# A depthwise convolution as banded products over four phases of time, with its norm and the projection's operand order moved

## The reference

```python
# second layer, after h = rmsnorm(x) * (1 + scale) + shift
proj = h @ w_in                       # q, k, v, index q/k/w, and cu (2 x 512 channels)
attn_out = _dsa_attention(q, k, v, q_idx, k_idx, w_idx)   # top-256 sparse, causal, 8 heads
a, g = split(cu); glu = a * sigmoid(g)                     # 512 channels
y = depthwise_conv(glu, conv_w, taps=31, causal) + conv_b  # y[t,c] = sum_k w[k,c] glu[t-30+k,c]
conv_out = silu(layernorm(y) * conv_norm_g + conv_norm_b)
x = x + gate * (concat([attn_out, conv_out]) @ w_out)      # then the feed-forward part
```

## Time and profile before

| | us |
|---|---|
| median of 3 runs (2816.2 to 2828.43) | 2823.13 |
| the profiled execution's own time | 2835.03 |
| its span, first to last instruction | 2833.4 |
| PE busy in the span | 2692.5 (95%) |
| PE weight loads | 2125.8 (75%) |
| DVE busy | 1351.5 (48%) |
| ACT busy | 844.7 (30%) |
| POOL busy | 258.5 (9%) |
| part of the chain that ended last which is on PE | 86% |

### The profile page before, as it was taken

One profiled execution on the slowest core, in us unless ns is written; L12 is line 12 of the kernel. 1 busy time (PEld: TensorE's weight loads), 2 busy tenths in 40 slices (PEclk: granted clock), 3 DMA queues, 4 the chain that ended last, 5 costly groups with the idle time before them and its releaser, 6 DMA issues.

```text
span 2833.4 us, 28934 instructions
## 1 busy us (share of the span) xinstructions
PE 2692.5 (95%) x11519; PEld 2125.8 (75%) x11519; DVE 1351.5 (48%) x1602; ACT 844.7 (30%) x1114; POOL 258.5 (9%) x267
## 2 busy tenths in 40 slices
PE   5999999999999999999998989999899999999996
PEld 3887667877888888888765767666678888888885
DVE  5242557356434343346748885787453232232233
ACT  3211344323212021122325574544333021120221
POOL 0000212102112121121001001110000000000000
PEclk9999789999999999999899999999999999999997
DMA  3211011113222222221310100000201111111111
GB/s 114 82 45 56 33 41 45 60 67 141 90 76 95 74 89 81 77 102 62 132 34 8 45 30 23 1 1 8 89 31 51 53 45 53 45 52 52 45 52 67
DMA packets 45255, 166.24 MB, mean 59 GB/s; under 512 B 5751, under 2 KB 6007, under 8 KB 45111
## 3 DMA queue, kind: packets, MB, share of 16 engines
q1 hardware_dynamic: 27936, 101.07, 10.1%
q0 software_dynamic: 17216, 63.72, 6.4%
HBM read 151.80 MB, written 12.68 MB: 58 GB/s over the span
## 4 chain that ended last, share of the span: by engine, by line
PE 86%; DVE 7%; ACT 4%; issue 3%; DMA 0%; POOL 0%; DVEq 0%; SPq 0%; ACTq 0%; POOLq 0%
PE G L1144 63%; PE G L1162 4%; PE TP L1569 2%; PE G L1338 2%; PE TP L1504 2%; PE G L1504 1%; PE TP L1358 1%; PE G L1485 1%; PE TP L1311 1%; ACT TK L994 1%; PE TP L1182 1%; PE TP L1205 1%; PE TP L1455 1%; ACT T L980 1%; PE TP L1537 1%
## 5 line engine op out<-in xcount | busy, mean ns | idle before, releaser
L1144 PE MATMUL G<-XH,whi 128*128 128x512 f32 x1712 | 539.3, 396 | 17.1 <-DVE wlo L1638 15.1
L1144 PE MATMUL G<-XH,wlo 128*128 128x512 f32 x1712 | 530.2, 391 | 0.0
L1144 PE MATMUL G<-XL,whi 128*128 128x512 f32 x1712 | 530.1, 391 | 0.0
L697 ACT ACTIVATE whi<-raw 128x1024 fp32r<-128x1024 f32 x184 | 193.8, 1053 | 730.8 <-PE G L1144 670.8
L1144 PEld LDWEIGHTS G<-XH,whi 128*128 128x128 f32 x1712 | 320.3, 189 | 89.2 <-DVE wlo L1638 19.2
L1144 PEld LDWEIGHTS G<-XL,whi 128*128 128x128 f32 x1712 | 323.3, 189 | 68.3
L1144 PEld LDWEIGHTS G<-XH,wlo 128*128 128x128 f32 x1712 | 322.9, 189 | 68.0
L1144 PE MATMUL G<-UH,whi 128*128 128x512 f32 x1024 | 316.7, 390 | 0.0
L1144 PE MATMUL G<-UL,whi 128*128 128x512 f32 x1024 | 315.3, 389 | 0.0
L1144 PE MATMUL G<-UH,wlo 128*128 128x512 f32 x1024 | 315.3, 389 | 0.0
L1638 DVE TENSOR_TENSOR wlo<-raw,whi 128x1024 fp32r<-128x1024 f32 x184 | 224.4, 1220 | 140.1 <-ACT whi L697 139.8
(11 more groups left out here) (307 smaller groups left out, 3315.5 us busy)
## 6 DMA issues: line engine op xcount, KB each, us to landing
raw<-slabs SPq DMA_DIRECT2D x184, 512.0 KB, 3.4
ADA<-ada POOLq DMA_DIRECT2D x48, 512.0 KB, 3.8
x_spill<-XT POOLq DMA_DIRECT2D x2, 4096.0 KB, 12.9
BIAS<-tab_spill POOLq DMA_DIRECT2D x8, 960.0 KB, 4.8
XT<-xT SPq DMA_DIRECT2D x8, 512.0 KB, 10.7
XRE<-xT POOLq DMA_DIRECT2D x8, 512.0 KB, 3.8
XRE<-x_spill POOLq DMA_DIRECT2D x8, 512.0 KB, 3.5
XT<-x_spill POOLq DMA_DIRECT2D x1, 4096.0 KB, 13.9
```

The costliest lines, as they stand in the source:

```text
L697: act.activation(whi[b][:, :, :].rearrange("p k n -> p (k n)"), raw[b][:, :], ACT.Copy).then_inc(hi_ready, 1)
L1144: last = pe.matmul(G[b][:, half, :], w[b][:, k, :], x[:, k, half * HALF:(half + 1) * HALF], start=(at_k == 0 and n == 0), stop=(at_k == KT ...
```

## The change

Time is written as 4u + phase. A new operand `XP` holds, for one group of 32 channels, four phases on the four groups of 32 partitions; a banded weight matrix `BAND` (128 x 9 x 128) maps four input phases to four output phases for a block of lags. Per tile there are 4 groups of channels and 9 blocks, so 36 products of 256 columns, in plain float32 without hi/lo split. All four tiles go to PE.

- PE: 36 products of tile 0 behind slabs 15 to 18 (9 behind each), 108 for tiles 1 to 3 spread over steps 3 to 57, two a step.
- DVE: no taps; instead `phases(j)`, 16 copies of 32 partitions x 256 for each tile, from a source with a stride of four; `band(n)`, 16 products of 128 x 1152 elements; one copy of the weight table.
- ACT: 20 very small copies early in the kernel, `phase_weights` (16 copies of 32 x 124) after the search of slab 11, `conv_result` (four instructions of 32 x 256 for each of 16 groups) in place of the diagonals, the splits and two results.
- POOL: one memset in place of 16 diagonal builds; its load of `XT` waits for the phases instead of the taps.
- The norm: means at step 62, squares from step 65, statistics at step 70, root at step 71, where they stood at the end. Silu and the operands of tiles 4 to 7 come before those of tiles 0 to 3, and `product_pair` takes the slices in that order.
- `hi` and `lo` of the first two slabs of `OUT2` move: from the projection's end and the middle of the attention to steps 59 and 60, since `BAND` uses their place.

```diff
-        for c in range(8):
-            first, n = 4 * c, min(4, CONV_K - 4 * c)
...
-                pool.tensor_tensor(DGC0[:, c % 4, which, 0:n, :], ident.unsqueeze(1).broadcast_to([P, n, P]),
-                                   w.unsqueeze(2).broadcast_to([P, n, P]), ALU.mult).then_inc(diag0_ready, 1)
+        pool.memset(WT[0][:, :, :, :], 0.0).then_inc(wt_zero, 1)
...
+        def phase_weights():
+            act.wait_ge(wt_zero, 1)
+            for q in range(PHASES):
+                for g in range(PHASES):
+                    first = PHASES + 1 - q
+                    w = vec[CB * g:CB * (g + 1), VCOL["conv_w"]:VCOL["conv_w"] + 4 * CONV_K].rearrange("p (j k) -> p j k", j=4)
+                    act.activation(WT[0][CB * q:CB * (q + 1), :, g, first:first + CONV_K], w, ACT.Copy).then_inc(wt_ready, 1)
+        def conv_result(n):
+            j, g = divmod(n, PHASES)
+            act.wait_ge(conv_used, (n | 1) + 1)
...
+            out = (Gf[1] if j else TPf[1])[:, g * S // PHASES:(g + 1) * S // PHASES]
+            for at_p in range(PHASES):
+                rows = slice(CB * at_p, CB * (at_p + 1))
+                act.activation(YC[CB * g:CB * (g + 1), j, PHASES - 1 - at_p::PHASES], out[rows, :], ACT.Identity,
+                               bias=phase_b[rows, 4 * g + j:4 * g + j + 1]).then_inc(conv_out, 1)
...
+            if m >= 17:
+                conv_result(m - 17)
+            if m == 11:
+                act.wait_ge(eye_ready, 5 * PHASES)
+                phase_weights()
...
-        conv_result(0, TPf[1])
-        conv_hi(1)
-        make_diagonals(4)
+        conv_result(2)
+        conv_result(3)
...
-            if n >= len(STEPS) - 4:
-                conv_square(n - len(STEPS) + 4)
+            if SQUARES_FROM <= n < SQUARES_FROM + 4:
+                conv_square(n - SQUARES_FROM)
+            if n == STAT_AT + 1:
+                norm_root()
...
-        norm_root()
         for j in range(4):
             t_hf.wait(act, 1)
...
             act.activation(XH[:, 4 + j, :], HC[j % 2][:, :], ACT.Copy).then_inc(x_hi, 1)
+        act.wait_ge(att2_scaled, 2 * len(UNITS2))
+        for k in range(4):
+            act.activation(XH[:, k, :], QT2[:, k, :], ACT.Copy).then_inc(x_hi, 1)
...
-            for n, (w, x) in enumerate(((hi_w, CUH), (hi_w, CUL), (lo_w, CUH))):
-                for half in range(2):
-                    last = pe.matmul(out[:, half, :], w, x[:, tap + half * HALF:tap + (half + 1) * HALF],
-                                     start=(tap == 0 and n == 0), stop=(tap == CONV_K - 1 and n == 2))
+        def conv_product(n, block):
+            j, g = divmod(n, PHASES)
+            if block == 0:
+                pe.wait_ge(band_ready, n + 1)
+                pe.wait_ge(phases_ready, PHASES * PHASES * (j + 1))
...
+                if j > 1:
+                    pe.wait_ge(conv_out, PHASES * ((n - PHASES | 1) + 1))
+            out = (Gf[1] if j else TPf[1])[:, g * S // PHASES:(g + 1) * S // PHASES]
+            ins = pe.matmul(out, BAND[2 * (j > 0) + n % 2][:, PHASES * block:PHASES * (block + 1), :].rearrange("p e c -> p (e c)"),
+                            XP[j % 2][:, g, block:block + S // PHASES], start=(block == 0), stop=(block == BLOCKS - 1))
...
-            for tap in range(4 * TAPS_BESIDE, CONV_K):
-                conv_tap(0, tap, TP[1])
...
-                if n == last_step[len(UNITS2) - 2] + PV_BEHIND:
+                if n == MEANS_AT:
                     conv_means()
-                if n == len(STEPS) + PV_BEHIND - 1:
+                if n == STAT_AT:
                     norm_stat(4, SSQ2, G[1])
...
-        product_pair(OUT2, XH, XL, x_split, 32)
+        product_pair(OUT2, XH, XL, x_split, 32, order=(4, 5, 6, 7, 0, 1, 2, 3))
...
+        def phases(j):
+            dve.wait_ge(glu_ready, j + 1)
...
+            if j > 1:
+                dve.wait_ge(conv_used, PHASES * (j - 1))
+            for q in range(PHASES):
+                for g in range(PHASES):
+                    dve.tensor_copy(XP[j % 2][CB * q:CB * (q + 1), g, :],
+                                    CU[CB * g:CB * (g + 1), j, q::PHASES]).then_inc(phases_ready, 1)
+        def band(n):
+            j, g = divmod(n, PHASES)
...
+            if n == PHASES:
+                dve.wait_ge(slab_done, 1 + OUT2)
+                dve.tensor_copy(WT[1][:, :, :, :], WT[0][:, :, :, :]).then_inc(wt_moved, 1)
+                dve.wait_ge(wt_moved, 1)
+            if n % PHASES >= 2 or n >= PHASES + 2:
+                dve.wait_ge(conv_used, n - 1)
+            dve.tensor_tensor(BAND[2 * (j > 0) + n % 2][:, :, :], eye[:, :].unsqueeze(1).broadcast_to([P, PHASES * BLOCKS, CB]),
+                              WT[j > 0][:, j, g, :].unsqueeze(2).broadcast_to([P, PHASES * BLOCKS, CB]), ALU.mult).then_inc(band_ready, 1)
...
+            if 16 <= m < 18:
+                band(m - 14)
...
+            if m == 13:
+                phases(0)
             if m == 14:
-                conv_low(0)
+                band(0)
+                band(1)
+            if m == 16:
+                phases(1)
...
         query_low(0)
+        band(4)
         key_low(1)
         query_low(1)
+        band(5)
...
-                    ins = dve.scalar_tensor_tensor(out=YC[:, j, :], in0=src, scalar=w, in1=YC[:, j, :], op0=ALU.mult,
-                                                   op1=ALU.add)
+        bands, tiles_due = list(range(PHASES + 2, PE_GROUPS)), list(range(2, PE_TILES))
+        def conv_due(step):
+            while bands and conv_end(bands[0] - 2) + 1 <= step:
+                band(bands.pop(0))
+            while tiles_due and conv_end(PHASES * (tiles_due[0] - 1) - 1) + 1 <= step:
+                phases(tiles_due.pop(0))
```

More of the change, by code:

```diff
@@ L37 @@
 CONV_K = 31
-PAD = CONV_K - 1
+PAD = 32
+LEAD = PAD - (CONV_K - 1)
+PHASES = 4
+CB = P // PHASES
+BLOCKS = -(-(CONV_K + PHASES - 1) // PHASES)
+N_BLOCK = S // PHASES + BLOCKS - 1
 SGU_G = 8
@@ L298, in build @@
     above_mag = small("above_mag", NQ)
[L299 to L300 removed]
+    eye = small("eye", CB)
+    phase_b = small("phase_b", 4 * PHASES)
     raw_loaded = [sem(f"raw_loaded{b}") for b in range(2)]
@@ L386, in least_out, with conv_by, conv_end @@
         return TPf[0][:, (p % 2) * HALF:(p % 2) * HALF + (i + 1) * P] if i < 4 else TPf[0][:, 0:(i + 1) * P]
-    TAPS_BESIDE = 4
-    def taps1_by(n):
-        return min((n + 1) * CONV_K // 64, CONV_K)
-    dve_taps = [(j, tap) for j in (2, 3) for tap in range(CONV_K)]
-    TAPS_OF_UNIT = [1, 1, 0, 2, 1, 4, 1, 5, 2, 6, 3, 8, 4, 9, 15, 0]
-    assert sum(TAPS_OF_UNIT) == len(dve_taps)
+    PE_TILES = 4
+    PE_GROUPS = PHASES * PE_TILES
+    FIRST_STEP, CONV_STEPS = 3, 54
+    def conv_by(n):
+        total = BLOCKS * (PE_GROUPS - PHASES)
+        return min(max(total * (n + 1 - FIRST_STEP) // CONV_STEPS, 0), total)
+    def conv_end(n):
+        return FIRST_STEP + CONV_STEPS * (n + 1 - PHASES) / (PE_GROUPS - PHASES)
     ACT_TILES, DVE_TILES = (1, 2, 5), (0, 3, 4)
@@ L1105, in _ @@
                 sums_inverse(u)
-        act.wait_ge(att2_scaled, 2 * len(UNITS2))
-        for k in range(4):
-            act.activation(XH[:, k, :], QT2[:, k, :], ACT.Copy).then_inc(x_hi, 1)
-        norm_root()
         for j in range(4):
@@ L1513, in _ @@
                     pe.wait_ge(v2_ready, 2)
-                for tap in range(TAPS_BESIDE * (m - 15), TAPS_BESIDE * (m - 14)):
-                    conv_tap(0, tap, TP[1])
+                for block in range(BLOCKS):
+                    conv_product(m - 15, block)
             if 6 <= m <= 10:
@@ L1593, in sparse_attention @@
                     scores_by_key2(n)
-                    for tap in range(taps1_by(n - 1), taps1_by(n)):
-                        conv_tap(1, tap, G[1])
+                    for k in range(conv_by(n - 1), conv_by(n)):
+                        conv_product(PHASES + k // BLOCKS, k % BLOCKS)
                 if n >= PV_BEHIND:
@@ L2158, in _ @@
         dve.wait_ge(pool_seq, 2)
-        tap_done = {}
-        def conv_taps(first, end):
-            for k in range(first, end):
-                j, tap = dve_taps[k]
-                w = V("conv_w", j * CONV_K + tap)
-                src = CU[:, j, tap:tap + S]
-                if tap == 0:
-                    dve.wait_ge(conv_used, CONV_K)
-                    ins = dve.tensor_scalar(YC[:, j, :], src, w, V("conv_b", j), ALU.mult, ALU.add)
-                else:
-                    dve.wait_ge(dve_seq, tap_done[j])
-                    ins = dve.scalar_tensor_tensor(out=YC[:, j, :], in0=src, scalar=w, in1=YC[:, j, :], op0=ALU.mult,
-                                                   op1=ALU.add)
-                if (j, tap) == (3, CONV_K - 1):
-                    ins.then_inc(conv_ready, 1)
-                else:
-                    d.inc(ins)
-                    tap_done[j] = d.n
+        bands, tiles_due = list(range(PHASES + 2, PE_GROUPS)), list(range(2, PE_TILES))
[4 more added lines that the diff above has]
```

(9 more changed lines are left out.)

123 lines of the change are left out of this document (45 added, 78 removed).

## The result

The changed kernel is slower by 0.7%: median 2843.26 us of 5 runs (2834.66 to 2854.79) against 2820.23 (2816.2 to 2828.43, 5 runs) for the kernel before, ratio 1.0071 with a 95% interval of 1.0040 to 1.0102. So the loss is 0.4 to 0.7%. I had predicted no change, 2823, and 0.18 for slower.

What follows compares the result with a forecast made beforehand. PE, holding 86% of the chain, was taken as the bound. From the profiled 2835.0 us, -6.0 to first scores, +10.5 in the attention and -4.4 in the tail gave 2835.1; against the median, 2823 was predicted, range 2807 to 2842.

Steps and rivals of the forecast that it cites:

- Rival B: New products on PE don't stream: 0.32 us a record, not 0.216, mainly in the attention; 2851 us; chance 0.15.
- 6.0 reach the path: Up to the first scores: of 27.7 us that tile 0 frees on PE, 6.0 shorten the path; bounds 11 and 2.
- the bound of 0.42: DVE's strided copies: upper bound of 0.42 us each, from a reduction of 256; 6.7 us for 16 copies.
- the forecast of 45 us: Slab 15 to slab 18: PE's period falls from 16.5 us to 14.8, three times.
- about 2.2 us of 5.0 show: Attention, step 3: `phases(2)` follows the reductions, PE has some 3 us of cover, so 2.2 us of stall.
- 3.4: Attention, unit 8: band 9 and `phases(3)` (6.3 us) ahead of two reductions, 2.9 us of PE cover; 3.4 us stall.
- Back come waits ... I take 3.4.: Attention: of PE's 7.9 us idle before `least`, 3.4 us return as waits where a tap lay ahead of a reduction.
- Bands: Attention: band 14, due after the reduction of step 47 and needed at step 48, costs PE 1.5 us.
- the exponential at steps 58 to 60: Attention: ACT has an inverse, two results, two `hi` and the exponentials against 1.8 us steps; 2.0 us of stall.
- the tail: Last value product to end of the output pair: 33.0 us instead of 37.4, gain 4.4 us; bounds 7 and 1.
- C: Rival: DVE's blocks weigh more; copies at 0.42 us add 1.9 in each of four blocks, +7.6, 2831; chance 0.2.
- The three upper bounds: Slow ends for the path to first scores (-2), the attention (+22) and the tail (-1), together +19 us.

Runs made afterwards that it cites:

- x1: Changed kernel with one contiguous copy per tile in place of the 16 strided copies, rearrangement into phases left out; 2814.5 us, ratio 0.9973 to the kernel before.
- x3: Changed kernel, all work done, copies of tiles 2 and 3 taken two at a time behind each reduction; 2824.3 us, ratio 1.0024 to the kernel before.
- x9: Changed kernel with 20 extra unread products in PE's idle time ahead of the first least products; 2837.4 us, ratio 1.0054 to the kernel before.
- c3: Changed kernel with copies spread and shared, DVE/ACT reordered, tile 1's products early, ACT's result instructions taken singly; 2797.9 us, ratio 0.9932 to the kernel before.

## Why the prediction was wrong

**Right: PE.** A plain float32 product of 256 columns costs 0.43 us: nine last 4.05 with the end of the last. Rival B, 0.32 a record, is out. Removed and added work on PE were sized well, but for a slip of 0.4 us: by the prediction's own 43.3 us for a tile of taps the attention gets 3.4 us more, not 3.0.

**Wrong step: "6.0 reach the path".** Only 0.2 us did: the first scores come 151.8 us behind the common point, where it was 152.0. Slab 15 is 2.4 us later than forecast, slabs 15 to 18 take 2.5 more, and the way to the scores 1.0 more. The chain was the right one; its terms on DVE and ACT were too cheap, as follows.

**Mis-sized: the small instructions.** I took 0.31 us a copy, and the bound of 0.42 was the truth: 6.63 us for 16, and 8.13 where POOL scales beside it. The weight table took 5.24 instead of 4.6; the line through the two copies in the earlier trace rows (1.07 us for 1024 columns, 3.63 for 4096) gives 0.32 us for one of 124 columns and 5.1 for 16, so the 0.27 was a slip. These are +1.6 and +0.6 of the 2.4 us by which slab 15 is later than forecast. Of the 2.5 us in slabs 15 to 18, `phases(1)` (6.71) costs 0.9: slab 18 starts 15.66 us behind slab 17, and 14.78 where the copies are left out (x1). The rest is slab 15, which lasts 13.35 us and not 10.9 behind PE's 9.3 us of idle time, at a clock of 0.81 over its 13.4 us and 1.00 for slab 16. In the kernel before it was slow too (12.65 us at 0.86, so that the three periods were 51.2 us and not three times 16.5), and the forecast of 45 us, three periods of 14.8 and 0.6 more, had little room for that. A result took 2.9 us instead of 1.6, because I took the slope of contiguous copies for an instruction that writes with a stride of four.

**Wrong step: "about 2.2 us of 5.0 show" and "3.4" for the two blocks in the attention.** They show 4.00 and 6.86. The chain of the argument was right, the place as well; I had taken the copies too cheap and the cover too long. The experiment that spreads them takes 11.6 us off, where I had 5.6: 9.2 of waits and 2.3 of PE's own work, as the clock stays up. For that second part the forecast had no term.

**Wrong step: "Back come waits ... I take 3.4."** Nothing came back. With the blocks gone PE waits 9.8 us for `least_col` (8.7 where the copies are left out), about as long as when the taps stood there (9.4). That fits a wait of two reductions in a row with one buffer, in which the taps had no part; but bands and copies stand where the taps stood, and no run leaves that place empty, so the reason is argued and only the missing gain is shown. It was the term with the weakest ground, a guess at what part of the earlier trace rows was inherent.

**Smaller.** Bands 2.9 (1.5 forecast), the exponential at steps 58 to 60 4.5 (2.0). The waits for diagonals, 3.4 us before, went, which I had not counted. PE's work in the attention grew by 7.6 us (205.1 to 212.7), not 4.8; 2.3 of the rest goes with the spread copies (210.4), where the clock is 0.98 instead of 0.96. Copies 5.3, waits that didn't return 3.4, exponential 2.5, bands 1.4, PE's time 2.8, less 3.2 for the diagonals, are 12.2 of the 13.0 us missed in the attention.

**Right: the tail.** 4.1 us gained, 4.4 forecast. The table loads are there, three behind the root, as the timeline of ACT shows:

```profile
1983.75 1.28 ACT L715 ACT_TABLE_LOAD   x1
...
1987.18 1.28 ACT L1073 ACT_TABLE_LOAD   x1
1988.48 0.63 ACT L1073 ACTIVATE OL<-OL 64x512 f32<-64x512 f32 x1
1989.12 1.28 ACT L1076 ACT_TABLE_LOAD   x1
1990.42 0.63 ACT L1076 ACTIVATE INV<-OL 64x512 f32<-64x512 f32 x1
1991.07 1.28 ACT L1120 ACT_TABLE_LOAD   x1
```

The next instruction starts 1.29 to 1.30 us after each load began (for the first and the last, which are not shown, at 1985.05 and 1992.36). The Trainium skill, ScalarE: Activation LUTs (What ACT_TABLE_LOAD costs), adds a drain of 1.38 us to each; no such time stands beside these four, and the measurement decides.

**Rivals.** C named the right mechanism and price ("copies at 0.42 us"), with +7.6 us for four blocks. It had 0.2, of which I put only a fifth over the bound. Its 7.6 us are close to what the price of the copies explains (1.6 ahead of slab 15, 0.9 up to slab 18, 5.3 in the attention); the other 11 us of the miss it did not have. The range held 2842 and the median was 2843.26, and 2834.93 when run again. What was missing is not a case but weight: several small terms, each taken near its cheap end, all fell on one side. The three upper bounds of the prediction add up to +19 us, and +19.1 was measured, but that is luck: the attention (23.5) and what tile 0 frees (0.2) lie beyond their bounds of 22 and 2, and the tail, 3.1 us better than its bound of 1, makes up for them.

The Trainium skill, VectorE: DVE Perf Modes (What auto-detection actually checks), names no stride among the conditions under which such a copy runs at two elements a cycle. The strided copies took 0.384 us and the contiguous ones 0.283 to 0.289, so the stride counts here, and the estimate of 0.29 us that I worked out from the page's formula fits the contiguous form alone.

## What to carry to other kernels

Work that is taken off the bounding engine and given to others as many small instructions is to be priced by where it stands in their queues: a block of a band and 16 copies (7.9 us) ahead of a reduction made PE wait 6.9 us, and with the copies of both blocks spread between reductions PE waited 1.1 us longer in all than without them (9.8 against 8.7). Take the price of an unseen form from the upper row when form and row differ in stride, and let a wait come back in the sum only where something shows that the removed work caused it. When idle time of the bounding engine remains, move its own work there: 15.6 us of products put into such a gap took 12.7 us off the attention and 8.3 off the whole stretch, since the first scores came 3.1 us later and the tail grew by 1.3.

## What the runs showed of the hardware

- A DVE copy of 32x264 float32 with a stride of four on the read side lasts 0.384 us, a contiguous one 0.283 to 0.289, on the same or on other partitions; sixteen contiguous ones last 3.73 us on their own partitions and 5.09 to others, 0.23 and 0.32 each.
- ACT: 32x256 from PSUM with a bias lasts 0.466 us with a contiguous destination and 0.712 with a stride of four.
- Three of the 16 copies of `phases(2)` took 0.8 to 0.9 us instead of 0.385, in the changed kernel, and only in the set beside which POOL's `scale_unit` ran (L663: 1.5 us from 1760.65 and from 1765.33 us; none of its work lies beside `phases(3)`, whose copies were all at 0.385). In x3, where the copies lie elsewhere, seven took 0.75 to 0.92 us; all seven ran while an instruction of `scale_unit` did, and no other copy did. So the slow copies go with POOL's work; what it is in it that slows them was not tried.
- Two executions of one kernel differed by 3.5 us in the stretch; PE's busy time in the attention was 3.8 us longer in the slower one, on the same 769 instructions, at a mean granted clock of 0.94 and not 0.96.
- PE that was busy 10.9 of the 12.9 us up to the first scores (x9), or 17.9 of 19.0 (c3), had its half clock behind them all the same (0.50 over 6.4 us, 0.53 over 10.3).
